# Six layers in split fp32: the second block's weight splits, recurrence steps and turnings of rows placed elsewhere between its products

## The reference

```python
def hybrid_layer(...):
    h = rmsnorm(x, norm_mix)
    (a_x, a_b, a_c, d_q, d_k, d_v, i_q, i_k, i_w,
     g_q, g_f, g_i, g_g, m_q, gate_logits) = split_cols(h @ w_in)
    y_a = a_b * causal_conv3(a_c * a_x, conv_w)
    ...
    y_b = dsa_attention(q, k, d_v, iq, ik, iw).reshape(b, s, DSA_HEADS * DSA_HEAD_DIM)
    hq = jax.nn.silu(g_q).reshape(b, s, HG_HEADS, HG_DK)
    ...
    log_f = jnp.logaddexp(jnp.log(lbh), jnp.log1p(-lbh) + jax.nn.log_sigmoid(zf))
    hk = -jnp.expm1(log_f)
    hv = g_i.reshape(b, s, HG_HEADS, HG_DV)
    o_c = hgrn2_chunkwise(hq, hk, hv, log_f).astype(x.dtype)
    o_c = rmsnorm(o_c, hgrn_out_norm) * jax.nn.silu(g_g.reshape(b, s, HG_HEADS, HG_DV))
    ...
    y_m = jnp.einsum('bhsm,bmhd->bshd', mp, mv).reshape(b, s, MEM_HEADS * MEM_HEAD_DIM)
    gates = jax.nn.sigmoid(gate_logits).reshape(b, s, N_BRANCH, D_MODEL)
    merged = gates[:, :, 0] * (branches[0] @ w_lift[0])
    for n in range(1, N_BRANCH):
        merged = merged + gates[:, :, n] * (branches[n] @ w_lift[n])
    x = x + merged @ w_out
    ...
    return x + (jax.nn.silu(gate) * up) @ ffn_w_down
```

## Time and profile before

| what | value |
|---|---|
| runs | 2529.51, 2531.7, 2532.35 us (median 2531.7) |
| the profiled execution's own time | 2531.49 us |
| its span | 2529.6 us, mean granted clock 0.993 |
| busy | PE 96%, weight loads 80%, DVE 61%, ACT 46%, POOL 4% of the span |
| chain that ended last | PE 86%, DVE 8%, ACT 3%, issue 2%, DMA 1% |
| second block, layer 0 / layer 1 | about 1415 to 1965 us / 1965 to 2530 us |

### The profile page before, as it was taken

How to read it: one execution, slowest core, us unless ns; L and a number is a source line. 1 busy time by engine, 2 the same in 40 slices (tenths; PEclk the granted TensorE clock), 3 DMA queues, 4 the chain that set the end, 5 groups by cost and what they waited for, 6 DMA issues and landing times.

```text
span 2529.6 us, 30989 instructions
## 1 busy us (share of the span) xinstructions
PE 2438.2 (96%) x12352; PEld 2035.4 (80%) x12352; DVE 1541.7 (61%) x2286; ACT 1173.1 (46%) x1625; POOL 107.9 (4%) x138
## 2 busy tenths in 40 slices
PE   6999999999999999998999999999999999989999
PEld 5788888887888878887888877887888878877887
DVE  6854655546546575567755676666555675666644
ACT  4644454444443454436434454463444454553442
POOL 2100000000000000000100100000100000000000
PEclk9999999999999999999999999999999999989999
DMA  7355352341754436543654335353754433444652
GB/s 241 113 209 200 133 200 101 133 167 54 254 176 167 166 102 248 183 151 123 246 199 151 129 133 200 117 200 125 266 200 160 170 116 135 152 148 155 234 177 92
DMA packets 263117, 418.91 MB, mean 166 GB/s; under 512 B 12192, under 2 KB 149408, under 8 KB 262976
## 3 DMA queue, kind: packets, MB, share of 16 engines
q1 hardware_dynamic: 258112, 400.15, 45.2%
q0 software_dynamic: 4864, 16.80, 1.8%
HBM read 415.86 MB, written 1.05 MB: 165 GB/s over the span
## 4 chain that ended last, share of the span: by engine, by line
PE 86%; DVE 8%; ACT 3%; issue 2%; DMA 1%; POOL 0%; SPq 0%; DVEq 0%; ACTq 0%
PE bank_L L1937 38%; PE bank_L L1921 18%; PE bank_S L2131 7%; PE bank_O L2131 7%; PE bank_L L1918 3%; PE bank_O L2070 2%; DVE wlo L1235 2%; DVE sm L1588 1%; PE bank_T L2058 1%; PE bank_T L2114 1%; ACT whi L950 1%; DVE pts L1611 1%; PE bank_S L1921 1%; PE bank_O L1921 1%; PE bank_T L1880 1%
## 5 line engine op out<-in xcount | busy, mean ns | idle before, releaser
L1235 DVE TENSOR_TENSOR wlo<-raw,whi 128x2048 fp32r<-128x2048 f32 (+1 forms) x332 | 712.2, 2169 | 291.1 <-ACT whi L950 290.1
L950 ACT ACTIVATE whi<-raw 128x2048 fp32r<-128x2048 f32 (+1 forms) x332 | 593.6, 1817 | 59.0 <-DMA raw<-in_w_in 24.1
L1937 PE MATMUL bank_L<-whi,xt_hi 128*128 128x512 f32 x1440 | 571.4, 397 | 9.1 <-DVE wlo L1235 7.5
L1937 PE MATMUL bank_L<-wlo,xt_hi 128*128 128x512 f32 x1440 | 563.1, 391 | 0.0
L1937 PE MATMUL bank_L<-whi,xt_lo 128*128 128x512 f32 x1440 | 562.4, 391 | 0.0
L1921 PE MATMUL bank_L<-whi,xt_hi 128*128 128x512 f32 (+1 forms) x800 | 314.8, 393 | 14.4 <-DVE wlo L1235 14.4
L1937 PEld LDWEIGHTS bank_L<-whi,xt_hi 128*128 128x128 f32 x1440 | 271.6, 189 | 65.3 <-issue 8.8
L1937 PEld LDWEIGHTS bank_L<-wlo,xt_hi 128*128 128x128 f32 x1440 | 271.3, 188 | 58.0
L1937 PEld LDWEIGHTS bank_L<-whi,xt_lo 128*128 128x128 f32 x1440 | 271.7, 189 | 53.6
L1116 ACT ACTIVATE tok<-bank_L 128x256 f32<-128x256 f32 x132 | 50.7, 384 | 568.0 <-PE bank_L L1937 568.0
L1921 PE MATMUL bank_L<-wlo,xt_hi 128*128 128x512 f32 (+1 forms) x800 | 309.3, 387 | 0.0
(11 more groups left out here) (311 smaller groups left out, 3248.9 us busy)
## 6 DMA issues: line engine op xcount, KB each, us to landing
raw<-in_w_gate_up SPq DMA_DIRECT2D x176, 512.0 KB, 5.7
raw<-in_w_in SPq DMA_DIRECT2D x72, 1024.0 KB, 6.0
draw<-in_w_down SPq DMA_DIRECT2D x44, 1024.0 KB, 5.9
raw<-in_ffn_w_up SPq DMA_DIRECT2D x88, 512.0 KB, 5.6
raw<-in_b_w_qkv SPq DMA_DIRECT2D x36, 1024.0 KB, 7.0
draw<-in_ffn_w_down SPq DMA_DIRECT2D x22, 1024.0 KB, 5.9
raw<-in_w_lift SPq DMA_DIRECT2D x32, 512.0 KB, 4.6
raw<-in_a_w_qkv SPq DMA_DIRECT2D x12, 1024.0 KB, 8.4
```

Source lines behind the costliest of these rows:

```text
L950: act.activation(wide(whi, w, nkc, ncols)[:, ks, :], wide(raw, w, nkc, ncols)[:, ks, :], ACT.Copy) \
L1235: dve.tensor_tensor(wide(wlo, w, nkc, ncols)[:, ks, :], wide(raw, w, nkc, ncols)[:, ks, :], wide(whi, w, nkc, ncols)[:, ks, :].bitcast(F32 ...
L1937: mm = pe.matmul(banks[bank][:, :], xx[:, k, t * P:(t + 1) * P], ww[:, k, :], start=(k == 0 and q == 0), stop=(k == KC - 1 and q == 2))
```

## The change

No computation is added or removed. Six edits of order:

1. `split_at` puts the half splits inside attentions one step later: steps 1 and 4 of 7, and 1, 3, 6 and 8 of 11.
2. The turning of yb (branch 1's result) moves into gate_00, its two groups ahead of the fourth and fifth of the eight row blocks of the second half; `inside` carries it. ACT makes `yt_hi` between the gate's two evacuations, DVE `yt_lo` behind the next split.
3. The convolution now stands ahead of gate_00's stage on DVE, its last multiplication behind it in a stage of its own (`conv_gate`); the weights of lift_11 are split ahead.
4. Around q: the weights of gate_01 are split ahead of q's stage, those of lift_01 ahead of lift_00's stage; `decay_sums` goes behind lift_00, `decays` behind lift_01.
5. The turning of hyc (branch 2's result) moves into gate_21 in the same way, and the second lift set is split ahead.
6. In `lifts` DVE splits the first half of w_out's set, adds the lifts of tokens 0 to 127 to r, and splits the second half only then.

```diff
--- before.py
+++ after.py
@@ -226,9 +226,10 @@
             add("gains", rows=rows, after=after)
             n["gb"] += len(rows)
-        def split(src, ready, dst, nkc=KC):
+        def split(src, ready, dst, nkc=KC, inside=False):
             st = add("split", src=src, ready=ready, dst=dst, nkc=nkc)
+            st["deferred"] = inside
             n["tp"] += nkc // 2
             n["sg"] += nkc // 2
             return (tlo_done, [[st["at"]["sg"] + k // 2 + 1 for k in range(nkc)]] * T, dst)
@@ -269,9 +270,9 @@
             return (tlo_done, [[st["at"]["sg"] + 2 * t + k // 4 + 1 for k in range(KC)] for t in range(T)], (xt_hi, xt_lo))
         def linear(lhs, loads, ncols, evac, nkc=KC, turned=False, func=ACT.Copy, narrow=None, after=(),
-                   into=LB, mid=None, **kw):
-
-            st = add("linear", lhs=lhs, ncols=ncols, nkc=nkc, turned=turned, evac=evac, w=n["w"], mid=mid,
+                   into=LB, mid=None, inside=None, **kw):
+
+            st = add("linear", lhs=lhs, ncols=ncols, nkc=nkc, turned=turned, evac=evac, w=n["w"], mid=mid, inside=inside,
                      func=func, narrow=narrow, after=after, into=into, **kw)
             chunks.append((loads, nkc, ncols))
             for t in range(T):
@@ -593,9 +594,9 @@
             def w_cols(c0, width=NW):
                 return [(0, cols(w_in[l], c0, c0 + width))]
-            def gate(branch, half, dst):
-
-                linear(lhs, w_cols(C_GATE + branch * D + half * NW), NW, "act", dst=dst, func=ACT.Sigmoid,
+            def gate(branch, half, dst, inside=None):
+
+                linear(lhs, w_cols(C_GATE + branch * D + half * NW), NW, "act", dst=dst, func=ACT.Sigmoid, inside=inside,
                        after=[(dev, n["dev"]), (rope_done, n["rope"])])
                 return (dst, n["aev"])
@@ -672,11 +673,14 @@
                 units.append(dict(rows=rows, dv=HD, sink=None))
             o_is = attention(units, HD ** -0.5, [(aev, small_ok[1])], (turn_done, n["turn"]), [], in_twos=True, fill=fill,
                              ps=ps2)
-            gate_00 = gate(0, 0, tc)
+            ylhs = split(yb, o_is, (yt_hi, yt_lo), nkc=4, inside=True)
+            yb_split = stages[-1]
             add("conv", l=l, after=conv_in)
+            gate_00 = gate(0, 0, tc, inside=yb_split)
+            add("ahead", w=n["w"] + 1)
+            add("conv_gate")
             n["conv"] += 1
             conv_used = (conv_done, n["conv"])
-            ylhs = split(yb, o_is, (yt_hi, yt_lo), nkc=4)
             lift(1, ylhs, 0, gate_0)
             lift(1, ylhs, 1, gate_1)
             add("conv_end", after=(lin_done, n["lin"]))
@@ -690,13 +694,15 @@
             counts = (n["hga"], n["hgd"], n["hgp"])
             add("ahead", w=n["w"] + 1)
             add("decay_logs", l=l, counts=counts, aev_z=n["aev"])
+            add("ahead", w=n["w"] + 2)
             linear(lhs, w_cols(C_GQ), NW, "act", turned=True, dst=hq, func=ACT.Silu, after=[])
             aev_q = n["aev"]
+            add("ahead", w=n["w"] + 2)
+            lift(0, ylhs, 0, gate_00)
             add("decay_sums", l=l, counts=counts)
-            lift(0, ylhs, 0, gate_00)
-            add("decays", l=l, counts=counts)
             gate_01 = gate(0, 1, tb)
             lift(0, ylhs, 1, gate_01)
+            add("decays", l=l, counts=counts)
             linear(lhs, w_cols(C_GI), NW, "act", dst=hv, after=[(dev, n["dev"])])
             add("decayed", l=l, counts=counts, aev_q=aev_q)
             linear(lhs, w_cols(C_GG), NW, "act", dst=hgate, func=ACT.Silu, after=[(dev, n["dev"])])
@@ -711,8 +717,9 @@
             n["hgp"] += T + 3 + T
             y_ok = headnorm(hyc.rearrange("p t (h d) -> p t h d", d=128), 4, 128, gains[:, l, 128:256],
                             (hg_act, n["hga"]), gate=hgate.rearrange("p t (h d) -> p t h d", d=128))
-            gate_1 = gate(2, 1, tb)
-            ylhs = split(hyc, y_ok, (yt_hi, yt_lo), nkc=4)
+            ylhs = split(hyc, y_ok, (yt_hi, yt_lo), nkc=4, inside=True)
+            gate_1 = gate(2, 1, tb, inside=stages[-1])
+            add("ahead", w=n["w"] + 1)
             lhs = rows_of(r, [(dev, n["dev"] + 2 + 2 * t) for t in range(T)])
             add("lifts", lhs=ylhs, rows=second[0], held=(gate_0, gate_1), w=n["w"])
             for half in range(2):
@@ -758,7 +765,7 @@
             for q, st in enumerate(fill):
                 for h in range(2):
-                    if i == (2 * q + h) * steps // (2 * len(fill)):
+                    if i == 1 + (2 * q + h) * (steps - 1) // (2 * len(fill)):
                         return [st["w"] + 1, (h,)]
             return None
@@ -1018,6 +1025,9 @@
                         evacuated(st, 0, LB[0])
                         if st["mid"]:
                             rows_hi(st["mid"], 0)
+                        if st["inside"]:
+                            group_hi(st["inside"], 0)
+                            group_hi(st["inside"], 1)
                         evacuated(st, 1, LB[1])
                 elif st["kind"] == "lifts":
                     split_upto(st["w"] + 2)
@@ -1441,6 +1451,9 @@
                     if st["mid"]:
                         rows_lo(st["mid"], 0)
                     split_upto(st["w"] + 1)
+                    if st["inside"]:
+                        group_lo(st["inside"], 0)
+                        group_lo(st["inside"], 1)
                     for t in range(T):
                         if st["evac"] == "bias":
                             biased(st, t, LB[t])
@@ -1448,9 +1461,11 @@
                             lifted(st["w"], t, st["half"], st["into"][t], (st["gate"], st["gate_is"]), st["first"])
                 elif st["kind"] == "lifts":
                     w = st["w"]
-                    split_upto(w + 2)
+                    split_upto(w + 1)
+                    split_lo(w + 2, (0,))
                     for half in range(2):
                         lifted(w + half, 0, half, (SB, OB)[half][0], st["held"][half])
+                    split_lo(w + 2, (1,))
                     lifted(w, 1, 0, SB[1], st["held"][0])
                     rows_lo(st["rows"], 0)
                     lifted(w + 1, 1, 1, OB[1], st["held"][1])
@@ -1737,6 +1752,7 @@
                                                               scalar=convw[:, st["l"], 2 - back, b:b + 1],
                                                               in1=y[:, b, back:SEQ], op0=ALU.mult, op1=ALU.add))
                         step.settle()
+                elif st["kind"] == "conv_gate":
                     dve.tensor_tensor(blk(3), blk(3), blk(2), ALU.mult).then_inc(conv_done, 1)
                 elif st["kind"] == "conv_end":
                     dve.wait_ge(*st["after"])
@@ -1907,6 +1923,8 @@
                         take(name)
                     if st["mid"] and t == 1 and k == 2:
                         turn_rows(st["mid"], 0)
+                    if st["inside"] and t == 1 and k in (3, 4):
+                        turn_group(st["inside"], k - 3)
                     for b, kk in [divmod(2 * k, nkc), divmod(2 * k + 1, nkc)] if st["turned"] else [(0, k)]:
                         if t == 0 and b == 0 and kk % 2 == 0:
                             pe.wait_ge(ready, max(v[kk + 1] for v in values))
```

## The result

The changed kernel takes 2510.14 us (median of 4 runs, 2505.91 to 2512.38), the kernel before 2530.61 us beside it (4 runs, 2528.68 to 2532.35). The ratio is 0.9917, 95% interval 0.9900 to 0.9935. 2510.4 had been forecast. The two intervals of runs don't touch, and the difference of 20.5 us is three times the widest spread of either kernel's four runs. The profiled execution of the changed kernel is its fastest, 2505.91 us with a span of 2503.4; that of before took 2531.49 us, span 2529.6.

A forecast was written before the change was run, and what follows sets the result against it. The prediction took TensorE (PE), busy 96% of the span, to bound the kernel. Terms of 4.55 us in layer 0 and 16.55 in layer 1 took 21.1 off 2531.49, giving 2510.4 us, range 2504 to 2518.

The forecast's parts named there:

- Part 1: Layer 1, z to v: weight splits ahead of the decay sums remove gate_01's long wait and half clock; 13.7 us gained.
- Part 2: Same place in layer 0: the 0.76 us wait ahead of gate_01 goes; 0.8 us gained.
- Part 3: Attention splits one step later end a 3.1 us wait: DSA gains 2.5 and 2.1 us, memory attention 0.2 per layer.
- Part 4: yb turned inside gate_00: 1.25 us gained per layer, with 0.6 given back waiting at z in layer 1.
- Part 5: hyc turned inside gate_21 delays w_out's load, eating the 2.4 us from its separated halves: -0.1 us per layer.
- (a): ACT becomes the bound at product g, each table switch costing its load's 1.28 us twice: 2523 us; chance 0.03.
- (d): Slower kernel: ACT's in-order high-half splits wait on late weight landings, ending over 2531.7 plus 5 us; chance 0.01.
- (b): Clock and small waits come out well: no late attention copies, no half clock at lifts; 2503 to 2506 us; chance 0.10.
- (c): Weights land late, so v or g waits 2 to 4 us with half clock again: 2514 to 2518 us; chance 0.12.
- (e): The change fails to work as described at gate_01, halving layer 1's chain gain: 2517 to 2519 us; chance 0.03.

The follow-up runs named there:

- edit 4 alone: Kernel before with only the weight splits moved ahead around q, decay_sums behind lift_00 and decays behind lift_01: 2517.29 us, ratio 0.9943.
- the extra exponentials: Changed kernel with repeated exponentials on ACT ahead of g's high-half split, one more in layer 0 and four in layer 1: 2513.24 us.

## Why the prediction was right, point by point

- **Part 1** (13.7): 13.67 in the trace, 13.6 with edit 4 alone. Its times along the chain hold as well: gate_01 at full clock in 11.14 us, no wait at v or g, slack of 1.3 at g (1.2 to 1.4 measured). One piece was off without consequence: the residual wait ahead of gate_01 is 0.76, not 0.6.
- **Part 2** (0.8): 1.02.
- **Part 3** (2.5 and 2.1, memory attention 0.2): 2.27, 2.20, and 0.25 and 0.37. Waits of 0.80 and 1.02 came where 0.9 and 1.0 were expected; the third, of 0.4, is 0.07 and 0.05, and in layer 0 the 0.28 of before stays, though part 3 counted 0.4 of small waits there as gone.
- **Part 4** (1.25 each, 0.6 given back at z in layer 1): 1.28 each, and 0.23 in both layers. (The terms given, 2.1 and 0.1 less 0.88, make 1.3.) The step "z's second half landed late" was mis-sized, and it was not the landing: ACT had the second high half done at 2168.88, but DVE took z's low halves only behind lift_10's sums, from 2167.28 to 2171.77. PE comes to the second half at 2171.76.
- **Part 5** (-0.1 each) is the part that was off. r comes 25.57 and 25.63 us after gate_21 where 26.0 was forecast, from an order of events that holds row by row (w_out is taken up 4.9 us after its issue, not 5.2). The waits were to be 1.7 and 3.5 to 4 and are 1.49 and 3.15 to 3.18. What failed is the sum behind it: the bounds took the clock as a gain of up to 1.5, the forecast took none, and layer 0 got 1.35 where -0.1 was forecast (layer 1: 0.23). It also called the pair of edits 5 and 6 "no gain" and left it there. The runs show two large terms of opposite sign, some 3.6 a layer for the halves and 2.4 to 3.6 against it for hyc inside.
- **The median.** 2510.4 against 2510.14 is closer than the reasoning was, and in part luck: the runs of the changed kernel alone spread over 6.5 us. Against the profiled execution it was 4.5 too high, mostly for two reasons: 2.8 from the untouched part with its two stretches of low clock, some 1.8 from part 5. The other three runs are slower by 4 to 6.5 us at lower mean clock.
- **The rivals.** (a) fell: table loads cost 1.28 us once here too, and ACT's row to g keeps its slack. (d) has its mechanism, as the extra exponentials show (4.36 us of ACT are 3.14 of PE), but no landing came late enough. (b) came in part, in the profiled run alone: behind the 3.15 at r in layer 0 the clock stays up. Its premise "waits of 1.07 leave the clock alone" doesn't hold in the trace it was read from: both stretches of low clock in the first block of before begin 0.2 to 0.3 us after such a wait. (c) and (e) didn't come: nothing waits at v or g, and gate_01 starts at 2199.96, which is 17.8 us after z's end, as forecast.

## What to carry to other kernels

When an engine with in-order work holds a piece that the next product needs, look at what long piece stands ahead of it and whether that piece has a later deadline: here moving the two recurrence stages behind one lift each was worth 13 of 20 us, and splitting earlier without it was worth nothing. Before hiding a small job inside a product, ask what is issued at that product's end; here 1.0 us of hidden transposes and the 1.5 us wait ahead of them delayed a 5 us load, which cost more than it hid, and two edits that belong together on paper had to be timed apart to see it.
